# Moving the later pieces of x, the unit matrix, the vectors and x itself from SyncE's and ScalarE's DMA queues to GpSimd's

## The reference, cut to what matters

```python
def rms_norm(x, g):
    y = x32 * rsqrt(mean(x32 * x32, axis=-1) + EPS)
    return y * g
def swiglu(x, w_gate, w_up, w_down):
    return (silu(x @ w_gate) * (x @ w_up)) @ w_down
# first block, first line:      x is (256, 1024), w_gate and w_up (1024, 2816), w_down (2816, 1024)
h = x + 0.5 * swiglu(rms_norm(x, ffn1_norm), ffn1_w_gate, ffn1_w_up, ffn1_w_down)
```

## Time and profile before

| what | value |
|---|---|
| median of 3 runs | 1213.48 us (1212.64 to 1214.53) |
| the profiled execution | 1214.66 us |
| its span in the profile | 1212.9 us |
| TensorE (PE) busy | 1203.3 us, 99% |
| VectorE (DVE) busy | 773.7 us, 64% |
| ScalarE (ACT) busy | 691.7 us, 57% |
| GpSimd (POOL) busy | 69.9 us, 6% |
| granted TensorE clock | 1.0 |
| DMA queues, share of 16 engines | q1 56.8%, q10 5.3%, q0 1.9% |

### The profile page before, as it was taken

How to read it: one execution, slowest core, us unless ns; L and a number is a source line. 1 busy time by engine, 2 the same in 40 slices (tenths; PEclk the granted TensorE clock), 3 DMA queues, 4 the chain that set the end, 5 groups by cost and what they waited for, 6 DMA issues and landing times.

```text
span 1212.9 us, 17120 instructions
## 1 busy us (share of the span) xinstructions
PE 1203.3 (99%) x5663; PEld 990.0 (82%) x5663; DVE 773.7 (64%) x1087; ACT 691.7 (57%) x1012; POOL 69.9 (6%) x119
## 2 busy tenths in 40 slices
PE   9999999999999999999999999999999999999998
PEld 7888888877788788888888788788888887888887
DVE  5665556687776565557678766665556666655554
ACT  6655555666555555557675576655555546655543
POOL 0430000000000000000220110000000001000000
PEclk9999999999999999999999999999999999999999
DMA  9977754544555999754655517986655444776771
GB/s 316 248 226 219 219 178 160 169 148 148 165 191 183 236 247 247 223 173 156 195 166 179 160 67 233 239 231 203 201 167 165 166 157 147 213 222 201 222 225 44
DMA packets 209553, 232.01 MB, mean 191 GB/s; under 512 B 56096, under 2 KB 150688, under 8 KB 209504
## 3 DMA queue, kind: packets, MB, share of 16 engines
q1 hardware_dynamic: 164960, 214.61, 56.8%
q10 hardware_dynamic: 42752, 11.02, 5.3%
q0 software_dynamic: 1792, 5.75, 1.9%
HBM read 219.78 MB, written 1.05 MB: 182 GB/s over the span
## 4 chain that ended last, share of the span: by engine, by line
PE 94%; DMA 2%; ACT 1%; DVE 1%; issue 0%; SPq 0%; ACTq 0%
PE bank L1952 29%; PE bank L1954 29%; PE bank L1953 29%; PE bank L2008 2%; DMA sb_probs<-sb_probs 2%; PE bank L2176 1%; PE bank L2192 1%; PE bank L2163 1%; DVE sb_wl L1309 0%; ACT sb_wh L729 0%; DMA sb_raw<-ffn_w_up 0%; PE bank L2161 0%; ACT sb_probs L1226 0%; ACT sb_probs L729 0%; PE bank L2038 0%
## 5 line engine op out<-in xcount | busy, mean ns | idle before, releaser
L1952 PE MATMUL bank<-sb_wh,sb_aTh 128*128 128x512 f32 (+1 forms) x1128 | 438.3, 389 | 1.0 <-DVE sb_wl L1309 0.9
L1954 PE MATMUL bank<-sb_wh,sb_aTl 128*128 128x512 f32 (+1 forms) x1128 | 432.8, 384 | 0.0
L1953 PE MATMUL bank<-sb_wl,sb_aTh 128*128 128x512 f32 (+1 forms) x1128 | 432.5, 383 | 0.0
L1309 DVE TENSOR_TENSOR sb_wl<-sb_raw,sb_wh 128x1024 fp32r<-128x1024 f32 x270 | 326.8, 1221 | 102.2 <-ACT sb_wh L729 97.9
L729 ACT ACTIVATE sb_wh<-sb_raw 128x1024 fp32r<-128x1024 f32 (+1 forms) x274 | 286.1, 1051 | 112.9 <-PE bank L1954 42.4
L1952 PEld LDWEIGHTS bank<-sb_wh,sb_aTh 128*128 128x128 f32 x1128 | 212.1, 188 | 43.3 <-issue 2.8
L1954 PEld LDWEIGHTS bank<-sb_wh,sb_aTl 128*128 128x128 f32 x1128 | 212.0, 188 | 42.2
L1953 PEld LDWEIGHTS bank<-sb_wl,sb_aTh 128*128 128x128 f32 x1128 | 212.3, 188 | 40.0
L1309 DVE TENSOR_TENSOR sb_wl<-sb_z,sb_wh 128x1024 fp32r<-128x1024 f32 x132 | 158.6, 1221 | 37.2 <-ACT sb_wh L729 37.1
L729 ACT ACTIVATE sb_wh<-sb_z 128x1024 fp32r<-128x1024 f32 x132 | 137.1, 1056 | 58.7 <-PE bank L1954 39.6
L1952 PE MATMUL bank<-sb_wh,sb_hTh 128*128 128x512 f32 x320 | 125.2, 391 | 1.7 <-DVE sb_hTl L1391 1.4
(11 more groups left out here) (217 smaller groups left out, 914.6 us busy)
## 6 DMA issues: line engine op xcount, KB each, us to landing
sb_raw<-w_in SPq DMA_DIRECT2D x80, 256.0 KB, 3.1
sb_z<-ffn_w_down SPq DMA_DIRECT2D x64, 256.0 KB, 4.6
sb_z<-w_down SPq DMA_DIRECT2D x64, 256.0 KB, 3.7
sb_raw<-w_gate SPq DMA_DIRECT2D x54, 256.0 KB, 3.5
sb_raw<-w_up SPq DMA_DIRECT2D x54, 256.0 KB, 4.3
sb_raw<-ffn_w_gate SPq DMA_DIRECT2D x52, 256.0 KB, 3.7
sb_raw<-ffn_w_up SPq DMA_DIRECT2D x52, 256.0 KB, 4.6
sb_raw<-e_w_in SPq DMA_DIRECT2D x40, 256.0 KB, 3.0
```

Source lines behind the costliest of these rows:

```text
L1309: dve.tensor_tensor(wl[:, u % NSPLIT, :], raws[SLOT[u]], wh[:, u % NSPLIT, :].bitcast(F32), ALU.subtract).then_inc(low_done, 1)
L1952: pe.matmul(dst, lh, w_hi, start=start, stop=False)
L1953: pe.matmul(dst, lh, w_lo, start=False, stop=False)
L1954: return pe.matmul(dst, ll, w_hi, start=False, stop=stop)
```

## The change

The three later pieces of xT, the unit matrix, the vectors and x are taken from SyncE's and ScalarE's programs and put into GpSimd's, between its constants and its first `token_rstd`. GpSimd waits until piece 0 has landed and issues pieces 2, 3 and 4; then it waits until TensorE has used two units and issues `ident`, `vecs` and the two halves of x. Semaphores, sizes and destinations are the same.

```diff
-            def load_xt(n, a, b):
-                sp.dma_start(xT[:, a:b, :], xt_piece(a, b)).then_inc(xt_in[n], 16)
-
             def load_front():
 
                 load_early_unit(0, 0)
                 load_early_unit(1, 1)
                 for u in range(2, 5):
-                    if u > 2:
-                        load_xt(u, 2 * u - 2, 2 * u)
                     load_gate_up(u, 0, FRONT[u][1], FRONT[u][0])
                 load_gate_up(5, 0, FRONT[5][1], FRONT[5][0])
-                sp.dma_start(ident[:], d["c_ident"]).then_inc(ident_in, 16)
-                sp.dma_start(vecs[:, KT:NCOL], d["h_vecs"][:, KT:NCOL]).then_inc(vecs_in, 16)
-                for t in range(NT):
-                    sp.dma_start(x[:, t, :], xv[:, t, :]).then_inc(x_in, 16)
                 for u in range(6, 8):
                     load_gate_up(u, 0, FRONT[u][1], FRONT[u][0])
...
+            pool.wait_ge(xt_in[0], 16)
+            for n in range(2, 5):
+                pool.dma_start(xT[:, 2 * n - 2:2 * n, :], xt_piece(2 * n - 2, 2 * n)).then_inc(xt_in[n], 16)
+
+            pool.wait_ge(units_used, 2)
+            pool.dma_start(ident[:], d["c_ident"]).then_inc(ident_in, 16)
+            pool.dma_start(vecs[:, KT:NCOL], d["h_vecs"][:, KT:NCOL]).then_inc(vecs_in, 16)
+            for t in range(NT):
+                pool.dma_start(x[:, t, :], xv[:, t, :]).then_inc(x_in, 16)
+
             token_rstd(0, 0)
...
             act.dma_start(xT[:, 0:1, :], xt_piece(0, 1)).then_inc(xt_in[0], 16)
             act.dma_start(xT[:, 1:2, :], xt_piece(1, 2)).then_inc(xt_in[1], 16)
-            act.dma_start(xT[:, 2:4, :], xt_piece(2, 4)).then_inc(xt_in[2], 16)
             load_tables(SILU_SET)
```

## The result

| | before | after |
|---|---|---|
| median of 13 runs | 1213.48 us (1212.62 to 1214.74) | 1217.44 us (1215.13 to 1220.03) |
| the profiled execution | 1214.66 us | 1216.06 us |
| its span | 1212.9 us | 1214.2 us |
| executions with a mean granted clock below 1.00 | none (of 47 shown beside the experiments) | 9 of 13 |

The ratio is 1.0029 (95% interval 1.0022 to 1.0037): slower by 0.3%, inside the stated range and on the forecast side. The move of the medians is +4.0 us (the ratio alone would make it 3.5 us), the forecast was +2.4 us.

A forecast was written before the change was run, and what follows sets the result against it. The prediction took the latest wait in TensorE's start, at units 2 and 6, as the bound. Its terms, 0 + 0 + max(1.3, 2.4) = +2.4 us, took the median from 1213.5 to 1215.9 us, range 1213.7 to 1219.5 us.

The forecast's parts named there:

- What bounds the kernel: TensorE's start: the latest wait at units 2 and 6 is handed to the end unchanged, with the DMA engines full.
- The parts at nothing: ScalarE's one DMA issue less, SyncE's six less, and ident and vecs through GpSimd: each worth 0.
- Unit 2, +1.3 us: At unit 2: pieces 2 to 4 through GpSimd make TensorE start it at 14.4 instead of 13.06 us.
- the bytes ahead: Ahead of unit 2's end: up to 0.52 MB more than before, worth up to 1.4 us.
- the second rival: GpSimd's first DMA is slow, piece 2 lands 7 us or more after issue: +3.7 us, 1217.2 us; 9%.
- x, landing at 21.9 us: At unit 6: x through GpSimd lands late, so TensorE gets unit 6 at 26.5 instead of 24.07 us, 2.4 us late.
- 1.5 us to the first bytes: In x's landing time: estimated wait from x's issue at 13.6 us to its first byte.
- an even share of 0.18 MB/us: In x's landing time: q0 gets half the bytes beside SyncE's queue, so x's 1.05 MB take 5.8 us.
- The rule of the Trainium skill: Engines take turns between queues, some 9 to 17 descriptors each; counted so, x gets four times the weights' bytes.
- the first rival: x is not late, landing at 19.8 us; only unit 2's loss is left: +0.4 to +1.4 us, 1214.6 us; 22%.
- The sum: Over all parts: 0 + 0 + max(1.3, 2.4) = +2.4 us, median 1215.9 us.
- the fourth rival: The gap ahead of unit 2 lets TensorE's clock fall; one unit at that pace costs 2.8 us: 1218.7 us; 3%.

The follow-up runs named there:

- e11: The changed kernel without GpSimd's wait for piece 0, so pieces 2 to 4 are issued from 1.8 us; median 1220.56 us.
- e1: The changed kernel with ident, vecs and x back on SyncE's queue, only pieces 2 to 4 through GpSimd; median 1217.17 us, ratio 1.0032.
- e7: The kernel before with pieces 2, 3 and 4 all issued by ScalarE; median 1215.45 us, ratio 1.0018.
- e5: The kernel before with x's two DMAs (4 KB rows) issued by ScalarE right before it waits for x; 1220.63 us in one execution.
- e6: The kernel before with x issued by ScalarE in four DMAs of 256 columns (1 KB rows); 1223.25 us in one execution.

## Why the prediction was right, and where not

**What bounds the kernel.** Right in the main point: x's landing sets unit 6 and the lateness at the start reaches the end. That all is handed through *unchanged* does not hold for single executions: between these two profiles the waits for a DMA transpose took back 1.4 us. The premise that the DMA engines move 350 GB/s throughout failed too, at 9 to 11 us (220 instead of 339 and 370 GB/s).

**The parts at nothing.** ScalarE's one issue less, SyncE's six less, ident and vecs: right. ident, issued at 12.4 us, took 6.0 us; nobody waited for it.

**Unit 2, +1.3 us.** Measured +1.41 us, and the closeness is in part luck. It compares one execution with one: over all profiles unit 2 starts at 12.05 to 13.14 us without the change to the pieces and at 14.3 to 15.2 us with the pieces on GpSimd's queue. And the bytes ahead, for which I allowed up to 1.4 us, are worth 0.5 us by the totals above; the rest came from the lower rate. Piece 2 landed at 10.97 us, between my 10.2 and 11.5 us, and unit 2's weights at about 12.0 us: both bounds are late. GpSimd's three issues ended at 6.86 us, not at 6.6 us "at the latest" (three of 0.91 us would have meant 7.2 us). GpSimd's first DMA was not slow beyond the others (5.9, 6.2 and near 8 us for the three), so the second rival, a slow first use of q0, did not come.

**x, landing at 21.9 us.** It landed at 22.2 us, but out of two wrong terms that cancel. I took 1.5 us to the first bytes; q0 was in full swing some 4.5 us after x's issue, at 18 us. GpSimd's rows that I read stood beside lighter traffic; that the new transfer waits behind what the engines have already been given would fit, but is not shown. And I took an even share of 0.18 MB/us; it was 0.29 to 0.31. The rule of the Trainium skill ("DMA: Bandwidth & Descriptors", Queues, rings and completion order) that I set against the earlier trace rows was the better guide: by it, as I worked it out, x gets four fifths of the bytes, and measured were 0.29 against 0.09 MB. The row that I read as an even share, 0.14 against 0.09 MB at 476 us, was never even in bytes: it has 41 packets beside 52, so it is nearer to equal packets, as is the other row with 167 beside 179. Had I taken the rule and kept my 1.5 us, I would have forecast the first rival, and been wrong.

**The price of a gap, the term that was too small.** The sum had nothing for TensorE's clock; the fourth rival had it with 3% and one cause, the gap ahead of unit 2. The runs show it in 9 of 13 executions, and in e11 the gap ahead of unit 6 is the one that does it. A fall costs 1.7 us in e1 and in e11, less than the rival's 2.8 us. It is most of the difference between +2.4 us forecast and +4.0 us measured: filler, which leaves the start as late as it is, gives +2.8 us. The argument against it, that the clock reads 1.00 in the profile before, spoke of gaps of 0.85 us and not of 2.4 us. That the measured time lies inside the range says little for this term: the sum came out 1.6 us too low.

**What I said would show it.** x on GpSimd's queue took 6.8 and 8.2 us, ScalarE waited 3.90 us for it, unit 2 was at 14.47 and unit 6 at 26.81 us (said: 7 us or more, over 3 us, 14.4 and 26.5). Two of the signs of being wrong came as well. A granted clock under 1 did, in other executions than the profiled one. And TensorE's idle time beyond 60 us changed, from 7.06 to 5.66 us; over all profiles of this case it lies between 5.7 and 7.9 us, without following how late the start is, so I take it for scatter.

## What to carry to other kernels

Where the DMA engines are full, a second queue is no second road: its transfers take their bytes from the first (here by packets, so that x's long ones took three to four times as many bytes), and whatever waited behind the first is late. A critical transfer that is triggered by progress has to be counted from its trigger to its first bytes beside a full queue (3 to 4 us here) and not from quiet rows. And a gap of 2 us on TensorE near the start can cost more than 2 us: look at the granted clock of every execution, since one profiled execution may miss it. Three short gaps (1.48, 0.44 and 1.01 us in e7) cost no clock in eleven executions, gaps of 2.37 and 1.18 us did in nine of thirteen.

## What the runs showed of the hardware that I had not expected

- While x travelled, two queues shared the DMA engines by packets: 87 packets to 89 with 4 KB against 1 KB rows on GpSimd's queue, 80 to 82 on ScalarE's, and 178 to 176 when both have 1 KB.
- A DMA issued beside a full queue moved nothing for 3 to 4 us, on ScalarE's queue (issued at 16.3 us, first bytes after 20 us) as on GpSimd's (ident issued at 12.4 us, first bytes at about 16 us).
- With GpSimd's pieces under way the DMA engines moved 220 GB/s at 9 to 11 us, though loads were waiting in SyncE's queue; with the same pieces on ScalarE's queue (e7) they moved 324 to 386 GB/s from 6 to 10 us.
- The clock fell when the gap was over: in e1 TensorE had been busy again for 0.4 us (15.18 to 15.6 us) when it went to 0.50, and it stayed there until 19 us with the engine fully busy. In e5 and e6, with gaps of 5.35 and 8.19 us, it fell within the gap.
